# Three transformer blocks on one core: block three's mixers put between the chunks of its projections, and block two's low parts moved from GpSimd to VectorE

## The reference

```python
# block two
u = x @ w_in_2                                  # conv value and gate, qkv, z, b and a
conv_out = silu(layer_norm(depthwise_conv_31(value * sigmoid(gate))))
qkv = silu(causal_depthwise_conv_4(qkv))        # then the gated delta rule in 8 heads
x = layer_norm(alpha * x + concat(conv_out, gdn_out) @ w_out_2)
x = layer_norm(alpha * x + (silu(g) * u2) @ w_down_2)

# block three
proj = x @ w_in_3                               # q_a k_a v_a q_i k_i w_i q_m k_m v_m o_m i_m f_m q_c k_c v_c
y_a = dsa_attention(q_a, k_a, v_a, q_i, k_i, w_i)   # 6 heads; 64 keys of 256 chosen by an indexer of 8 heads
qk_m = silu(causal_conv_4(concat(q_m, k_m)))
y_m = sigmoid(o_m) * head_rmsnorm(mlstm(q_m, k_m, v_m, i_m + b_i, f_m + b_f))   # 6 heads
y_c = head_rmsnorm(softmax(q1 k1) v - lam * softmax(q2 k2) v) * (1 - lam_init)  # 4 heads
x = layer_norm(alpha * x + concat(y_a, y_m, y_c) @ w_out_3)
x = layer_norm(alpha * x + square(relu(x @ w_up_3)) @ w_down_3)
```

## Time and profile before

| | |
|---|---|
| median of 3 runs | 3884.43 us (3882.35 to 3886.08) |
| profiled execution | 3886.59 us, its span 3884.4 us |
| PE busy | 3534.8 us (91%) |
| DVE busy | 2298.6 us (59%) |
| ACT busy | 1593.2 us (41%) |
| POOL busy | 229.3 us (6%) |
| granted TensorE clock, mean | 0.955 |
| chain that ended last | PE 81%, DVE 13%, issue 3%, ACT 2% |

### The profile page before, as it was taken

The page is one execution under the profiler, slowest core; times in us unless marked ns, Lnnn a source line. Parts: engine busy times, 40 slices in busy tenths (PEclk is TensorE's granted clock), DMA queues, the critical chain, the costliest instruction groups (busy, mean ns, idle before and its releaser), DMA issues.

```text
span 3884.4 us, 60446 instructions
## 1 busy us (share of the span) xinstructions
PE 3534.8 (91%) x24578; PEld 3302.7 (85%) x24578; DVE 2298.6 (59%) x2844; ACT 1593.2 (41%) x1924; POOL 229.3 (6%) x81
## 2 busy tenths in 40 slices
PE   8899999999999635789999999997988899999998
PEld 8898999999899525769999988796977689998886
DVE  6666544445639976565444457756545654445676
ACT  4345544444343231134333355532333344445554
POOL 0000000000028740000000000000000000000000
PEclk9999999999999867999999999998989899999999
DMA  6455555556566310055666656563434356665554
GB/s 194 120 163 152 169 180 179 174 174 209 164 183 176 93 39 1 22 173 181 182 183 181 181 175 193 173 196 89 146 105 130 122 183 183 183 179 176 193 191 154
DMA packets 324981, 606.38 MB, mean 156 GB/s; under 512 B 30579, under 2 KB 44917, under 8 KB 323524
## 3 DMA queue, kind: packets, MB, share of 16 engines
q1 hardware_dynamic: 318436, 584.86, 49.9%
q10 hardware_dynamic: 6368, 19.01, 1.3%
HBM read 601.69 MB, written 2.10 MB: 155 GB/s over the span
## 4 chain that ended last, share of the span: by engine, by line
PE 81%; DVE 13%; issue 3%; ACT 2%; DMA 1%; DVEq 0%; SPq 0%; ACTq 0%
PE ps L565 25%; PE ps L566 25%; PE ps L567 25%; DVE arena L1453 4%; DVE arena L1450 1%; DVE arena L1447 1%; DVE xtok L1453 1%; DVE w_lo L1447 1%; PE ps L964 1%; DMA ring<-in_w_in 1%; DVE arena L2061 1%; PE ps L975 1%; PE ps L972 1%; ACT w_hi L1079 1%; PE ps L808 0%
## 5 line engine op out<-in xcount | busy, mean ns | idle before, releaser
L1447 DVE TENSOR_TENSOR w_lo<-ring,w_hi 128x1024 fp32r<-128x1024 f32 (+3 forms) x1088 | 1296.4, 1196 | 1345.1 <-ACT w_hi L1079 1158.2
L1079 ACT ACTIVATE w_hi<-ring 128x1024 fp32r<-128x1024 f32 (+2 forms) x1160 | 1192.9, 1032 | 1731.2 <-PE ps L565 1675.6
L565 PE MATMUL ps<-x_hi,w_hi 128*128 128x256 f32 x5632 | 1609.5, 286 | 83.8 <-POOL w_lo L556 60.4
L566 PE MATMUL ps<-x_lo,w_hi 128*128 128x256 f32 x5632 | 1602.6, 285 | 0.0
L567 PE MATMUL ps<-x_hi,w_lo 128*128 128x256 f32 x5632 | 1602.0, 284 | 0.0
L565 PEld LDWEIGHTS ps<-x_hi,w_hi 128*128 128x128 f32 x5632 | 1085.0, 193 | 92.9 <-POOL w_lo L556 61.1
L566 PEld LDWEIGHTS ps<-x_lo,w_hi 128*128 128x128 f32 x5632 | 1085.2, 193 | 1.9 <-issue 0.2
L567 PEld LDWEIGHTS ps<-x_hi,w_lo 128*128 128x128 f32 x5632 | 1084.7, 193 | 1.6
L565 PE MATMUL ps<-w_hi,h_hi 128*128 128x512 f32 x864 | 338.0, 391 | 9.4 <-DVE h_lo L1447 9.4
L566 PE MATMUL ps<-w_lo,h_hi 128*128 128x512 f32 x864 | 337.4, 391 | 0.0
L567 PE MATMUL ps<-w_hi,h_lo 128*128 128x512 f32 x864 | 337.3, 390 | 0.0
(11 more groups left out here) (328 smaller groups left out, 3012.6 us busy)
## 6 DMA issues: line engine op xcount, KB each, us to landing
ring<-in_w_in SPq DMA_DIRECT2D x416, 512.0 KB, 3.7
ring<-in_w_down SPq DMA_DIRECT2D x216, 512.0 KB, 4.3
ring<-in_w_gate_up SPq DMA_DIRECT2D x176, 512.0 KB, 3.6
ring<-in_w_up SPq DMA_DIRECT2D x128, 512.0 KB, 3.7
ring<-in_w_out SPq DMA_DIRECT2D x64, 512.0 KB, 4.2
ring<-in_w_branch SPq DMA_DIRECT2D x36, 512.0 KB, 3.8
ring<-in_w_in SPq DMA_DIRECT2D x48, 384.0 KB, 3.3
ring<-in_w_o SPq DMA_DIRECT2D x32, 512.0 KB, 4.4
```

What stands on the lines that cost most here:

```text
L565: first = pe.matmul(out, left[0], right[0], start=start, stop=False)
L566: pe.matmul(out, left[0], right[1], start=False, stop=False)
L1079: last = act.activation(w_hi[:, s, :, 0:width], ring[:, s, :, 0:width], ACT.Copy)
L1447: return dve.tensor_tensor(o, a, b, op)
```

## The change

Block two: POOL's loop of low parts is removed. VectorE makes them, and `wide_conv` has become a generator of 16 steps (two taps of two channel groups each), one step behind each low part of the qkv and z tiles; the short convolution stays behind each tile. A semaphore of its own (`wide_order`) orders the chains. `conv_ready` now comes behind `pass_by("ba")`.

Block three: the sections are ordered qkm, qi, vm, qkc, vc, qka, va, om, then wout3. The narrow sections kwi and if are gone: their 84 columns (`kif_w`) are loaded by two DMAs ahead of the first qkm chunk, split once (`kif_hi` by ScalarE, `kif_lo` by VectorE), and multiplied by PE in four side steps. Three generators `third_mixers` (PE, ScalarE, VectorE) hold convolution, gates, indexer, selection, and the attention of mls, dif and dsa in this order, 120 steps behind 120 chunks. `attend`, `attention` and `softmax_exp` are removed; `attention_steps` and `exp_steps` now know all kinds. Buffers of the softmax are single and lie in the layer norm's parameter area, whose load moves behind om. The norm by head takes sums by token (a product of 1 column for each head and half), a root and a reciprocal of 12 or 8 numbers for each partition, and spreads them by a matmul with the identity. The output gate o_m is applied last. wout3 takes its chunks in the order of `MIXED`, so that the parts of y that are ready last come last.

```diff
-            for name in ("qkv", "z", "ba"):
-                sec = plan[name]
-                for t, u, it in tiles_of(pool, sec):
-                    for c in range(AHEAD, AHEAD + sec.chunks):
...
-                        pool.tensor_tensor(w_lo[:, s, :, 0:widths[g]], ring[:, s, :, 0:widths[g]],
-                                           w_hi[:, s, :, 0:widths[g]].bitcast(F32), ALU.subtract).then_inc(lo_ready[s], 1)
...
             def wide_conv(t):
...
-                        last.then_inc(dve_order, 1)
-                dve.wait_ge(dve_order, before + 2 * CONV_W)
+                        last.then_inc(wide_order, 1)
+                    if k % 2:
+                        yield
+                dve.wait_ge(wide_order, before + 2 * CONV_W)
+                yield
...
+            with n.loop(dve, sec.n // 2, {dve_order: 2 * 3, wide_order: 2 * CONV_W}) as i:
+                wide = wide_conv(2 * i)
                 for t, u in ((2 * i, sec.u0), (2 * i + 1, 1 - sec.u0)):
+                    for c in range(AHEAD, AHEAD + sec.chunks):
+                        split(sec.chunk(u, c), sec.more(i))
+                        next(wide)
+                    if u != sec.u0:
+                        next(wide, None)
                     dve.wait_ge(tile_free[u], sec.tiles[u] + i + 1)
...
-                wide_conv(2 * i)
-            wide_conv(6)
+            wide = wide_conv(6)
+            for t, u, it in tiles_of(dve, plan["z"]):
+                for c in range(AHEAD, AHEAD + plan["z"].chunks):
+                    split(plan["z"].chunk(u, c))
+                    next(wide)
+            next(wide, None)
+            pass_by("ba")
             dve.sem_inc(conv_ready, 1)
...
+            for col, width, at in ((C_KI, 72, 0), (C_IF, 12, 72)):
+                sp.dma_start(kif_w[:, :, at:at + width], w[:, col:col + width].rearrange("(k p) c -> p k c", p=P))\
+                  .then_inc(kif_landed, 16)
+            tile_loads("qkm", w, C_QM)
...
+                yield from attention_steps(mls.seq())
+                yield from spread_scales(0, m3_sq, M_H, 5)
+                yield
+                yield from attention_steps(dif.seq())
+                yield
+                yield from spread_scales(1, c3_sq, D_H, 6)
+                yield from attention_steps(dsa.seq())
...
+            def spread_scales(k, src, heads, at):
+
+                pe.wait_ge(sq3_ready, k + 1)
+                pe.wait_ge(o_used, n.now(o_used))
+                for h in range(heads):
+                    for t in range(2):
+                        last = pe.matmul(ps[:, at - 1 + k, 2 * h + t:2 * h + t + 1], src[:, h, t * P:(t + 1) * P], ones[:, 0:1],
+                                         start=True, stop=True)
+                last.then_inc(sums_ready, 1)
+                yield
+                yield
+                pe.wait_ge(scale_ready, k + 1)
+                for h in range(heads):
+                    for t in range(2):
+                        o = ps[:, at + h // 2, (h % 2) * S + t * P:(h % 2) * S + (t + 1) * P]
+                        last = pe.matmul(o, t_root[:, 2 * h + t:2 * h + t + 1].to_broadcast([P, P]), ident, start=True, stop=True)
+                last.then_inc(spread_ready, 1)
+                yield
...
+            side = third_mixers()
+            project_opening("qkm", side=side)
+            project("qi", "F", side=side)
+            project("vm", "T", width=384, side=side)
+            project("qkc", "F", side=side)
+            project("vc", "T", side=side)
+            project("qka", "F", side=side)
+            project("va", "T", width=384, side=side)
+            project("om", "F", width=384, side=side)
```

More of the change, by code:

```diff
@@ L136, in plan_weights @@
               ("gu", 2 * D_FF2 // TW), ("down2", 4)]
-    third = [("qka", 3), ("va", 2), ("qi", 1), ("kwi", 1), ("qkm", 3), ("vm", 2), ("om", 2), ("if", 1),
-             ("qkc", 2), ("vc", 1), ("wout3", 4), ("up3", D_FF3 // TW), ("down3", 4)]
+    third = [("qkm", 3), ("qi", 1), ("vm", 2), ("qkc", 2), ("vc", 1), ("qka", 3), ("va", 2), ("om", 2),
+             ("wout3", 4), ("up3", D_FF3 // TW), ("down3", 4)]
     order = first + second + third
@@ L463, in tile_loads @@
                     for c in range(sec.chunks):
-                        load(sec.chunk(u, c), sec.more(it), [w[rows(c), ds(at, width)]])
+                        load(sec.chunk(u, c), sec.more(it), [w[rows(c if order is None else order[c]), ds(at, width)]])
                         if after is not None and t == 0:
@@ L747, in attention_steps @@
                             pe.wait_ge(probsT_out, at[probsT_out] + outs(g))
+                        if not late and g:
+                            pe.wait_ge(o_used, at[o_used] + g)
                         for u in range(A.outs):
@@ L1414, in _ @@
-            act.wait_ge(vec_ready, n.next(vec_ready))
-            act.activation(e_sq[:, 0:4], e_cut, ACT.Square, scale=SHRINK).then_inc(sq_ready, 1)
-            roots(e_rn, D_H, 1.0 / P, eps_diff)
+                act.wait_ge(kif_landed, 32)
+                act.activation(kif_hi[:], kif_w, ACT.Copy).then_inc(kif_hi_ready, 1)
+            side = third_mixers()
+            for t, u, it in tiles_of(act, plan["qkm"], True):
+                splits(plan["qkm"], u, it, before=opening(t, third_rows), side=side if t else None)
@@ new lines, in conv_step @@
+            def conv_step(t, k):
+                sec = plan["qkm"]
+                u, count = sec.taken(t)
+                dve.wait_ge(tile_free[u], count)
+                for c in range(4):
+                    o, r, wk = m3_qk[:, 4 * t + c], e_raw[:, u, c, k:k + S], mcw[:, k, 4 * t + c:4 * t + c + 1]
+                    last = tsc(o, r, wk, ALU.mult) if k == 0 else stt(o, r, wk, o, ALU.mult, ALU.add)
+                if k < SHORT_W - 1:
+                    link(last)
+                else:
+                    last.then_inc(conv3_done, 1)
@@ L2008, in wide_conv @@
             def wide_conv(t):
[L2010 removed]
+                before = n.now(wide_order, 2 * CONV_W)
                 for k in range(CONV_W):
@@ L2128, in _ @@
             layer_norm("down2", hidden=True)
-            for k in range(SHORT_W):
-                last = dve.tensor_copy(mcw[:, k, :].rearrange("p (a t) -> p a t", a=2),
-                                       colp[:, 0:6, R_CM + 2 * k:R_CM + 2 * k + 2].rearrange("p t a -> p a t"))
-            link(last)
-            take("qka", e_qk, "F", before=opening)
-            take("va", e_v, "T", 384)
-            take("qi", i_q, "F")
-            pass_by("kwi")
-            u, count = plan["kwi"].taken(0)
@@ L2163, in _ @@
-            attention(dsa, float(P) ** -0.5, i_sel, y3[:, 0:6], slopes=slopes_a)
-            over()
-            dve.memset(e_raw[:, :, :, 0:RP], 0.0)
+            LAM0 = 0.8 - 0.6 * math.exp(0.0)
+            side = third_mixers()
             sec = plan["qkm"]
-            for t, u, it in tiles_of(dve, sec):
-                splits(sec, u, it)
-                dve.wait_ge(tile_done[u], sec.tiles[u] + t // 2 + 1)
+            for t, u, it in tiles_of(dve, sec, True):
+                splits(sec, u, it, before=opening(t), side=side if t else None)
+                dve.wait_ge(tile_done[u], sec.taken(t)[1])
@@ new lines, in _ @@
+            take("vm", m3_v, "T", 384, side=side)
+            take("qkc", c3_qk, "F", side=side)
+            take("vc", c3_v, "T", side=side)
+            take("qka", a3_qk, "F", side=side)
+            take("va", a3_v, "T", 384, side=side)
+            sec = plan["om"]
+            for t, u, it in tiles_of(dve, sec, True):
+                splits(sec, u, it, side=side)
+                dve.wait_ge(tile_free[u], sec.taken(t)[1])
+                v = y3[:, 6 + 3 * t:9 + 3 * t]
+                tt(v, v, e_gate[:, 3 * t:3 * t + 3], ALU.mult).then_inc(y3_ready, 1)
```

817 lines of the change are left out of this document (431 added, 386 removed).

## The result

The changed kernel takes 3721.71 us (median of 4 runs, 3720.16 to 3723.13), the kernel before 3883.39 beside it: ratio 0.9585, interval 0.9573 to 0.9597, 161.7 us less. The forecast was 3722. The total came out to the microsecond, but its two halves did not: block two gave 10 us more than the sum said and block three 8 us less.

| | before | after | gained | forecast |
|---|---|---|---|---|
| TensorE starts the sums over channels of block two | 1413.9 | 1361.9 | 52.0 | 44.2 |
| first transpose of block three | 2516.3 | 2462.4 | 53.9 | 44.2 |
| from there to the last residual add of its output projection | 613.4 | 502.3 | 111.1 | 119.1 |
| from there to the end | 754.7 | 756.0 | -1.3 | 0 |

What follows compares the result with a forecast made beforehand. VectorE, slowed by POOL, bounds block two; in block three TensorE alone sets projections, the PE, DVE, ACT chain the mixers. 3884.4 - 44.2 - 119.1 = 3721, stated as 3722 us, range 3702 to 3770.

Steps and rivals of the forecast that it cites:

- Rival B: Block two: POOL does not cause the slow convolution; stage ends near 1552, kernel takes 3903 us; chance 4%.
- the low part: Block two, VectorE: 61 full low parts at 1.25 us each with the gap, 76.3 us together.
- The bound of 19 us for dependent instructions at full duration: Block two: 240 convolution instructions at 476 ns instead of 397 would lose 19 us, leaving 25 gained.
- the 6.5 us of the formula: Block two: by the Trainium skill's formula, 424 ns each, the 240 instructions cost 6.5 us more; forecast 3728.
- The 12 us for ba: End of block two's stage: low parts of ba and the next three chunks before the convolution's semaphore, 12 us.
- The opening: Block three's start: the first tile with its transposes, 31.8 us.
- Hand-offs and the kif load: Block three: about eight hand-offs 8 us, loading kif_w 2 (between 0 and 10), late output projection 1.
- The granted clock at 1.0 from 2525 to the end: Block three, sign of being right: TensorE's granted clock stays at 1.0 through the output projection.
- a sign of being wrong: Block three: a drop of the clock in va or om would show the forecast wrong.
- TensorE's side work: Block three: head pairs, diff, indexer, biases, gate and index projection, norms between chunks; 57.2 us, bounds 50 to 65.
- The indexer's logits: Block three, TensorE side work: 1.27 us for two heads, eight heads 5.1 us.
- Rival A: Block three: hand-offs set the pace, some 45 steps at 1.3 us, 58 instead of 8; 3772 us; chance 12%.
- Rival C: Block three: the kif load delays the opening by its full 10 us; 3730 us; no chance of its own.

Runs made afterwards that it cites:

- the run alone: The kernel before with only block two's part of the change, block three as before: 3827.76 us, ratio 0.9863.

## Why the prediction was right, and where it was not

**What bounds.** Right in both stretches, in block two with one half missing: VectorE, held up by GpSimd; TensorE waiting inside the mixers of block three. The missing half is that VectorE's unbroken groups held GpSimd up as well. The group that the prediction took for undisturbed, with "hardly any POOL work left to do", ran beside a GpSimd instruction that stood for 20 us. As a price without GpSimd its 0.40 us came out right all the same. Rival B (the slow convolution is not GpSimd's doing) is refuted by the trace and, with the cause turned on again by itself, by the two runs with GpSimd beside.

**Block two, 44 us forecast, 52 (by the marks) to 55 (by the run alone) measured.** The mis-sized term is the low part: the 1.225 us of the earlier trace rows plus a gap was taken, 1.25, but in a full queue the next instruction starts 1.14 us after it. 61 x 0.11 = 6.7 of the 7.3 us by which VectorE's work from the first low part (1142.87) to the end of the convolution (1350.9) is shorter than 215.3. The same reading had been made correctly for the convolution, 397 ns between starts and not 476 of duration; it was not applied to the low part. The bound of 19 us for dependent instructions at full duration did not come about, nor did the 6.5 us of the formula: instructions of 128x256 stand 0.40 us apart, as in the earlier trace rows. The 12 us for ba came out as 12.0, from the third narrow part (1349.9) to the start of the sums. They were taken as given, and 5 of them need not be paid. The last 2 us, between the sums and block three, are scatter: this stretch, which the change leaves alone, took 1099.4 to 1102.4 us over the twelve traces, 1102.4 before and 1100.5 after.

**Block three, 119 us forecast, 111 measured.** Of the 415.0 us to the output projection (407.2 forecast):
- The opening, from the first transpose until VectorE takes the first tile (2493.57): 31.1, forecast 31.8.
- Hand-offs and the kif load: 11 us forecast (8 + 2 + 1), 9.9 measured, 9.7 of them in the table of waits. The load left TensorE 0.2 us late at a low part. Its price was read wrongly, and without consequence: in the slices of the earlier trace rows with 22 to 27 GB/s only 5 to 59 pieces moved in 0.75 us each, most bytes in pieces of 2 to 4 KB, while just ahead of them 1036 of 64 bytes moved in one slice. The 4096 pieces of kif were through in 5.3 us (2440.3 to 2445.6) and not 10.5. The waits are right in the sum, but the largest was put down at 1 us and is 3.2, behind table loads. And the 9.1 us taken for all of TensorE's waits in block one are its largest row; the same view has 11.6 in all.
- The clock: nothing was set, 5.9 us lost. 1.6 behind the wait for the gates, 1.0 behind the 1.9 us wait at L707 (not by this wait alone: in the two traces with the gates a step later it stands there too, and the clock behind it is 1.00), and 1.6 behind each group of sums by token. "The granted clock at 1.0 from 2525 to the end" was wrong in four places. This is the step that failed: every term was priced at 2.4 GHz, although the rows of before showed a lower clock wherever TensorE had idled, and although the change adds 20 products of one column. The run with 64 columns shows that half of it is these products. The second fall lies in va, which the prediction had named as a sign of being wrong.
- TensorE's side work: 57.2 forecast, 415.0 - 31.1 - 307.2 - 9.9 - 5.9 = 60.9 measured. Between the starts of its own products lie 54.1 us in the timeline. Another 4.4 are at the 50 changes from projection to side work, 0.21 us from start to start where 0.12 is usual, and some 2 more have no place that I can name. The indexer's logits were mis-sized: a chunk of vm with a head takes 3.16 us against 16.65 / 8 = 2.08 alone, 1.08 a head, and 0.64 was taken. Index and gate projection (5.6), biases (6.6) and norms (9.8) came within 0.3 of their terms. (The sum has a slip of 0.3: six pairs at 3.15 are 18.9 and not 19.2.)

Rival A (most hand-offs cost a microsecond) did not come about: some ten waits in 120 steps, 1 us each. Rival C, the load, cost 0.2.

That the total agreed to a microsecond is luck: the two errors against each other, +9.7 and -8.0, with 1.3 lost behind the output projection. The last is scatter as well: this stretch took 754.7 us in the trace of before and 755.1 to 756.5 in the eleven others, 756.5 in the one with block three as before. And the base of block three was itself 6 us above what another execution of the same instructions took: the kernel before has a spread there that a forecast from one trace inherits.

## What to carry to other kernels

Price an instruction in a full queue by the distance between starts, and read a group whose mean lies far above its undisturbed cost as a mixture of free and blocked instructions; here each of GpSimd's 3 us instructions cost VectorE 2.1 us. Then look at the other engine too: a group of VectorE without a break held a GpSimd instruction for 20 us and more, and TensorE behind it. When work is put in steps between the chunks of TensorE's main loop, expect the side work plus hand-offs (here 10 us on some 57), and look for the two or three steps that ask one step too early; moving those is cheap and kept TensorE at its higher clock here. A gain read from one execution carries that execution's luck, here 2 to 4 us, into every sum built on it. A semaphore that is posted behind unrelated work of the same engine is a wait that no busy time shows.

## What the runs showed that was not expected

- Beside VectorE's groups of 60 instructions GpSimd's low part of 128x1024 took 24.52 us and one of 128x32 took 20.60, until the group was through.
- 12 products of one column (24 records, 2.84 us, no idle time) are followed by products at the lower level: granted clock 0.79 in the stretch, 1.6 us lost. With 64 columns the group takes 2.89 us and the clock is 1.00. In one case of 16 the clock did not fall.
- A GpSimd subtraction of 128x1024 stretched one VectorE instruction from 0.47 to 2.61 us, and the low part under way when it began not at all. 32 such subtractions cost 68 us, 64 cost 134.
- The same six products behind the same wait of 2.45 us took 5.46 us in one execution and 2.81 in another, at a granted clock of 0.52 and 0.94. Code in which TensorE idles often is not only slow but uneven.
- One edit of position alone (the semaphore ahead of ba) sped up the 16 sums behind it from 6.5 to 3.6 us (granted clock 0.56 and 1.00), with no wait of TensorE ahead of them. It gained no more than half a microsecond, since VectorE's next step stood behind low parts: it starts 6.1 us after the first sum, where it was 6.6.
